# Two attentions of a twelve-stage block run as one sequence of places, with their heads' preparation put last in each place

## What is computed

```python
qa = (rmsnorm(cq, cq_gain) @ w_uq).reshape(lead + (8, 64 + 32))
kv = (rmsnorm(ckv, ckv_gain) @ w_ukv).reshape(lead + (8, 64 + 64))
ka = jnp.concatenate([kv[..., :64], kr_h], axis=-1)   # kr_h: kr for all 8 heads
qa, ka = rmsnorm(qa, q_gain), rmsnorm(ka, k_gain)      # "mla": 8 heads, 8 key heads
qb, kb = rmsnorm(gq, qg_gain), rmsnorm(gk, kg_gain)    # "gqa": 8 heads, 2 key heads
qa, ka = rope_tail(qa, 32, row, col), rope_tail(ka, 32, row, col)
oa = joint_dense_attention(qa, ka, va, kac, vac)       # 512 tokens see 768 keys
ob = joint_dense_attention(qb, kb, vb, kbc, vbc)       # context sees its 256
x = x + gate * ((concatenate([oa, ob]) * silu(g)) @ w_out)
```

## Time and profile before

| | us |
|---|---|
| median of 3 runs | 1555.17 (1554.95 to 1555.58) |
| the profiled execution, its own time | 1554.78 |
| its span | 1553.0 |
| PE busy | 1487.5 (96%) |
| DVE busy | 850.9 (55%) |
| ACT busy | 677.9 (44%) |
| POOL busy | 592.3 (38%) |
| chain that ended last, share by PE | 81% |

### The profile page before, as it was taken

How to read it: one execution, slowest core, us unless ns; L and a number is a source line. 1 busy time by engine, 2 the same in 40 slices (tenths; PEclk the granted TensorE clock), 3 DMA queues, 4 the chain that set the end, 5 groups by cost and what they waited for, 6 DMA issues and landing times.

```text
span 1553.0 us, 25078 instructions
## 1 busy us (share of the span) xinstructions
PE 1487.5 (96%) x9488; PEld 1240.5 (80%) x9488; DVE 850.9 (55%) x1879; ACT 677.9 (44%) x1377; POOL 592.3 (38%) x349
## 2 busy tenths in 40 slices
PE   4999998898999999999899999999999999999998
PEld 3778787787888878888788889967788788877887
DVE  4573708876764265933742997056322599617322
ACT  3333336565566353335744333467323433346332
POOL 1212223691005553447725444423234444430244
PEclk9999999999999999999999999999999999999999
DMA  9657620000012333331013323300233233310322
GB/s 326 181 140 192 175 62 27 2 2 1 2 35 89 108 109 96 95 95 42 28 33 94 96 82 98 93 14 28 69 93 106 75 99 101 96 41 1 109 82 95
DMA packets 103717, 128.61 MB, mean 83 GB/s; under 512 B 10608, under 2 KB 63792, under 8 KB 103600
## 3 DMA queue, kind: packets, MB, share of 16 engines
q1 hardware_dynamic: 103600, 127.01, 27.4%
HBM read 124.90 MB, written 2.10 MB: 82 GB/s over the span
## 4 chain that ended last, share of the span: by engine, by line
PE 81%; DVE 7%; POOL 5%; ACT 3%; issue 3%; DMA 1%; SPq 1%; DVEq 0%; ACTq 0%; POOLq 0%
PE psum L1048 21%; PE psum L1050 20%; PE psum L1049 20%; PE psum L1293 3%; PE psum L1236 3%; PE psum L1004 2%; PE psum L1215 2%; PE psum L1151 1%; PE psum L1340 1%; PE psum L1322 1%; PE psum L1272 1%; POOL rx L2403 1%; POOL mla_q L2403 1%; DVE psum L1943 1%; PE psum L1273 1%
## 5 line engine op out<-in xcount | busy, mean ns | idle before, releaser
L2353 POOL TENSOR_TENSOR wlo<-wraw,whi 128x1024 fp32r<-128x1024 f32 (+4 forms) x181 | 413.1, 2283 | 704.6 <-ACT whi L1445 704.6
L1445 ACT ACTIVATE whi<-wraw 128x1024 fp32r<-128x1024 f32 (+4 forms) x181 | 181.6, 1003 | 421.7 <-PE psum L1050 415.4
L1048 PE MATMUL psum<-whi,h2h 128*128 128x512 f32 (+2 forms) x800 | 309.5, 387 | 2.6 <-DVE h2l L1959 1.5
L1050 PE MATMUL psum<-whi,h2l 128*128 128x512 f32 (+2 forms) x800 | 305.2, 382 | 0.0
L1049 PE MATMUL psum<-wlo,h2h 128*128 128x512 f32 (+2 forms) x800 | 304.6, 381 | 0.0
L1048 PEld LDWEIGHTS psum<-whi,h2h 128*128 128x128 f32 x800 | 150.3, 188 | 28.5 <-issue 2.7
L1050 PEld LDWEIGHTS psum<-whi,h2l 128*128 128x128 f32 x800 | 150.2, 188 | 27.1
L1049 PEld LDWEIGHTS psum<-wlo,h2h 128*128 128x128 f32 x800 | 150.4, 188 | 24.8
L1048 PE MATMUL psum<-whi,hTh 128*128 128x512 f32 (+2 forms) x372 | 143.4, 385 | 3.7 <-DVE hTl L1959 2.7
L1050 PE MATMUL psum<-whi,hTl 128*128 128x512 f32 (+2 forms) x372 | 136.2, 366 | 0.0
L1049 PE MATMUL psum<-wlo,hTh 128*128 128x512 f32 (+2 forms) x372 | 135.8, 365 | 0.0
(11 more groups left out here) (391 smaller groups left out, 2956.4 us busy)
## 6 DMA issues: line engine op xcount, KB each, us to landing
rx<-mod_w_in SPq DMA_DIRECT2D x32, 512.0 KB, 5.1
wraw<-w_in_odd_in SPq DMA_DIRECT2D x32, 512.0 KB, 3.6
wraw<-cd_w_in_in SPq DMA_DIRECT2D x24, 512.0 KB, 3.7
wraw<-w_in_even_in SPq DMA_DIRECT2D x20, 512.0 KB, 3.7
wraw<-ab_w_out_in SPq DMA_DIRECT2D x16, 512.0 KB, 3.7
wraw<-w_ple_gate_in SPq DMA_DIRECT2D x16, 512.0 KB, 3.8
mod_w_even<-mod_w_in SPq DMA_DIRECT2D x8, 512.0 KB, 10.3
wraw<-ab_w_in_in SPq DMA_DIRECT2D x8, 512.0 KB, 8.3
```

Source lines behind the costliest of these rows:

```text
L1048: eng.matmul(dst, a[0], ww[0], start=first, stop=False)
L1050: mm = eng.matmul(dst, a[1], ww[0], start=False, stop=last_)
L1445: eng.activation(hi_of(u)[:, :, 0:w], wraw[:, u["id"] % RAW, :, 0:w], ACT.Copy).then_inc(*to("split_hi", u["id"]))
L2353: eng.tensor_tensor(lo_of(u)[:, :, 0:w], wraw[:, u["id"] % RAW, :, 0:w], f32(hi_of(u)[:, :, 0:w]), ALU.subtract)\
```

## The change

1. gqa and mla are one sequence: `places(*names)` gives 96 places and four more, and every engine's loop runs over it, so that mla's first scores stand where gqa's last probabilities are turned.
2. In a place ACT now does copy, exponential, then the high part of the preparation; DVE does maximum, copy, gate, inverse, then the low part, then `beside`. This holds for win too.
3. In mla's first block the preparations stand in places 3 to 10.
4. Key sums: POOL squares only the 64 columns that differ from head to head, in 12 half tiles with two buffers, and the shared 32 once; DVE sums two half tiles per place, behind the maximum. The key gain's first 64 columns are folded into the query gain, and POOL multiplies the keys by the gain in 32 columns only. Keys come before queries on POOL.
5. A key preparation of gqa waits only for the doubled keys, a query preparation for the queries; the first ones of mla wait for the tiles that they turn.
6. Modulation tiles 30 and 31 leave in1 for gqa's places 0 to 2.
7. diff, fox and odd wait for their values at their first product with them.
8. Slabs 0 to 3 of out3 and out4 are turned in fox and odd.
9. fox's scores use banks 0, 2 and 3 in turn. The second spread in win stands at place 6 instead of 9.

```diff
+        def mod_bank(n_):
+            return 6 if n_ == 31 else 7
...
         def mods_beside(n_):
-            return (2 * n_ - 8, 2 * n_ - 7) if 4 <= n_ < 4 + len(MOD) // 2 else ()
+            return mod_pair(n_) if n_ < 19 else ()
...
-                     ("win", 3): (1, 0, 0), ("win", 9): (1, 0, 1)}
+                     ("win", 3): (1, 0, 0), ("win", 6): (1, 0, 1)}
...
-        late_turns = {"fox": "m3", "odd": "m4"}
+        late_turns, EARLY_SLABS = {"fox": "m3", "odd": "m4"}, 4
...
-            groups = groups_of(late_turns[name], 0, 2)
+            groups = groups_of(late_turns[name], 0, EARLY_SLABS)
...
+        def places(*names):
+            return [(name, j) for name in names for j in range(len(units_of(name)) + 4 * (name == names[-1]))]
+        def product_of(place):
+            return place[0], place[1] // 2
...
+        def pair_scores(n_):
+            return 2 * (n_ % 2) if PAIR[n_][0] == "diff" else (0, 2, 3)[n_ % 3]
...
-                    when = first + (3 * before // 2 if name == "mla" else 2 + 2 * before)
+                    when = first + (max(3 * before // 2, 3 + before if first == 0 else 0) if name == "mla" else 2 + 2 * before)
...
# tensor
+            def start_modulation(j):
+                if j < 2:
+                    modulation_tile(30 + j)
+                if j > 0:
+                    turn_modulation(29 + j)
...
-                if p_[0] == prep_times(name)[-1][0][0]:
+                if name in STACKED and key[1] == 0:
+                    for w_ in [("keys_twice", (name, 1))] if key[0] == "k" else [("vector", ("normed", name[0] + "q", t)) for t in tiles]:
+                        eng.wait_ge(*at(*w_))
+                elif p_[0] == prep_times(name)[-1][0][0]:
...
+                if name == "mla" and key[1] == 0:
+                    for t in tiles:
+                        eng.wait_ge(*at("gpsimd", ("normed", "m" + key[0], t)))
...
# scalar, column_attention
-                for j in range(len(units) + 4):
+                for n_, (name, j) in enumerate(seq):
...
+                    if 2 <= n_ < len(seq) - 2:
+                        copy_probs(*seq[n_ - 2], turned_probs(*seq[n_ - 2]), product_of(seq[n_ - 5]) if n_ >= 5 else None)
+                    if j < len(units):
+                        if n_ >= 3:
+                            probs_free(*seq[n_ - 3])
+                        exponentials(name, j, probs(name, j))
                     for what in preps_at(name, j):
                         prep(*what)
-                    if 2 <= j < len(units) + 2:
-                        copy_probs(name, j - 2, turned_probs(name, j - 2), (name, (j - 5) // 2) if j >= 5 else None)
-                    if j < len(units):
-                        if j >= 3:
-                            probs_free(name, j - 3)
-                        exponentials(name, j, probs(name, j))
...
# vector: the low parts (`low`) move behind copy, gate and inverse in the same way
...
+            def reduce_keys(n_):
+                half_, t = divmod(n_, NT)
+                a = NT * 8 + t * 8 + half_ * 4
+                eng.wait_ge(*at("squares_g", ("mk", n_)))
+                after_last()
+                eng.tensor_reduce(ssq[:, a:a + 4], key_squares(n_), AX.X, ALU.add).then_inc(*note("vector", ("reduced", "mk", n_)))
...
# gpsimd, mla_norms
+                for n_ in range(2 * NT):
+                    half_, t = divmod(n_, NT)
+                    eng.wait_ge(*at("evac_act", (f"up{2 + half_}", t)))
+                    if n_ >= 2:
+                        eng.wait_ge(*at("vector", ("reduced", "mk", n_ - 2)))
...
-                for name, roots in (("mq", heads_rstd[:, 0:48]), ("mk", heads_rstd[:, 48:96])):
+                for name, roots in (("mk", heads_rstd[:, 48:96]), ("mq", heads_rstd[:, 0:48])):
```

More of the change, by code:

```diff
@@ L764, in heads_view, with key_squares @@
             return ap.rearrange("p (h d) -> p h d", h=h)
+        shared_squares = squares[:, 512:512 + NT * 32].rearrange("p (t d) -> p t d", t=NT)
+        def key_squares(n_):
+            return squares[:, n_ % 2 * 256:n_ % 2 * 256 + 256].rearrange("p (h d) -> p h d", h=4)
         norms = {
@@ L1194, in _ @@
             ready_of = {
-                "gqa": [("keys_twice", ("gqa", 1))] + [("vector", ("normed", "gq", t)) for t in ALL],
-                "mla": [("gpsimd", ("normed", n_, t)) for n_ in ("mq", "mk") for t in ALL] + [evac_of("up3", t) for t in ALL],
-                "win": [("keys_twice", ("win", 1))] + [("vector", ("normed", "wq", t)) for t in XT],
+                "mla": [evac_of("up3", t) for t in ALL],
                 "diff": [("vector", ("normed", n_, t)) for n_ in ("qa", "ka") for t in XT],
@@ L1244, in copies_ready, with column_attention @@
                     eng.wait_ge(*at("probs_b", (name, i)))
-            def column_attention(name):
-                units, preps = units_of(name), prep_times(name)
-                n_units, waited = len(units), set()
-                for j in range(n_units + 3):
-                    if j < n_units:
+            def column_attention(*names):
+                seq, waited = places(*names), {name: set() for name in names}
+                for n_, (name, j) in enumerate(seq[:-1]):
+                    units = units_of(name)
+                    if j < len(units):
                         h, t = units[j]
-                        wait_heads(name, j, waited)
+                        wait_heads(name, j, waited[name])
                         s0 = score_bank(j)
@@ L1345, in pair_attention @@
             def pair_attention():
-                for name in ("diff", "fox"):
-                    for n_ in values_of[name]:
-                        for t in XT:
-                            eng.wait_ge(*at(*evac_of(n_, t)))
                 waited = set()
@@ L1416, in _ @@
             products("up")
-            column_attention("gqa")
-            column_attention("mla")
+            column_attention("gqa", "mla")
             products("out1")
@@ L2104, in copy_probs, with column_attention @@
                 eng.tensor_copy(place[:, 0:nb * P], psum[:, 4, 0:nb * P]).then_inc(*note("probs_a", (name, i)))
-            def column_attention(name, beside=lambda j: None):
-                units, preps = units_of(name), prep_times(name)
-                for p_ in preps[-1] if name == "win" else ():
-                    first_head(name, p_)
-                for j in range(len(units) + 4):
-                    if j < len(units):
-                        maximum(name, j)
+            def column_attention(*names, beside):
+                seq = places(*names)
+                for p_ in prep_times("win")[-1] if "win" in names else ():
+                    first_head("win", p_)
+                for n_, (name, j) in enumerate(seq):
+                    if j < len(units_of(name)):
+                        maximum(name, j)
+                    if 2 <= n_ < len(seq) - 2:
+                        copy_probs(*seq[n_ - 2], turned_probs(*seq[n_ - 2]), product_of(seq[n_ - 5]) if n_ >= 5 else None)
+                    if n_ >= 5 and n_ % 2:
+                        name2, m = product_of(seq[n_ - 5])
+                        z = gate_columns(name2, m)
+                        eng.wait_ge(*at("product_v", (name2, m)))
+                        eng.tensor_tensor(z, psum[:, 6, P:2 * P], z, ALU.mult).then_inc(*small())
+                        after_last()
+                        eng.tensor_tensor(z, psum[:, 6, 0:P], z, ALU.mult).then_inc(*note("mixed", (name2, m)))
+                    if n_ >= 3 and n_ % 2 and n_ < len(seq) - 1:
+                        name2, m = product_of(seq[n_ - 3])
+                        eng.wait_ge(*at("exps", (name2, 2 * m + 1)))
+                        c_, r_ = 2 * m % 4, 2 * (m % 4)
+                        eng.reciprocal(rinv[:, r_:r_ + 2], rsum[:, c_:c_ + 2]).then_inc(*note("vector", ("inverse", name2, m)))
@@ L2124, in column_attention @@
[L2124 to L2129 removed]
+                    if name != "mla":
+                        beside(j)
             def attention(name):
@@ L2283, in _ @@
                     first_head("gqa", p_)
-            column_attention("gqa", mla_norms)
-            column_attention("mla")
+            column_attention("gqa", "mla", beside=mla_norms)
             products("out1", 0)
@@ L2306, in conv @@
                        .then_inc(*note("conv", ("lo", c)))
-            column_attention("win", conv)
+            column_attention("win", beside=conv)
             products("out2")
@@ L2402, in mla_norms @@
                         turned = t in XT
-                        eng.tensor_tensor(view(t), view(t), gg, ALU.mult).then_inc(*(small() if turned else note("gpsimd", ("normed", name, t))))
+                        part = view(t)[:, :, first:d]
+                        eng.tensor_tensor(part, part, gg, ALU.mult).then_inc(*(small() if turned else note("gpsimd", ("normed", name, t))))
                         if turned:
```

139 lines of the change are left out of this document (83 added, 56 removed).

## The result

| | us |
|---|---|
| before, median of 4 (lowest, highest) | 1555.38 (1554.95, 1555.97) |
| after, median of 4 (lowest, highest) | 1577.62 (1575.97, 1579.04) |
| ratio after/before, 95% interval | 1.0143 (1.0128 to 1.0159) |
| profiled execution of after, its span | 1575.97, 1574.1 |

The kernel became slower by 22.2 us. The sign is the one that I gave, and the chain through bank 7 is what the profile shows; but the size is twice what I gave (22.2 against 10.1), and 1577.6 lies outside the range of 1549 to 1574.

What follows compares the result with a forecast made beforehand. PE's instruction stream and its waits were taken to bound the kernel. Costs of 21.1 us less gains of 11.0 gave +10.1 on 1554.78, so 1564.9, against the median some 1565; range 1549 to 1574.

Steps and rivals of the forecast that it cites:

- the chain through bank 7: End of gqa and mla: each close preparation waits for the previous low part; costs 21.1 us, total 1565, chance 0.58.
- The eight preps: mla's first head preparations, in gqa's places 40 to 47: their starts spread from 16.35 to 23.3 us, costing +6.9.
- blocks two and three: mla's second and third block: three neighbouring pairs of preparations in each take longer, +3.6 per block, +7.2 together.
- the row of seam, copies and first block: From gqa's drain through mla's first block: seam -2.8, copies ahead of the low part -1.0, first block +7.0; +3.2 together.
- Rival B: gqa places 40 to 47: low parts not late enough to hold PE, kernel faster at 1543 us; chance 0.15.
- C: Part of both: early copies remove gqa's 3.9 us idle, start gains 4 more; 1557, down to 1551; chance 0.15.
- I take 0 for gqa's middle and win together, between -4 and +4: Preparations stand two or more places apart, bank 7 free in time; a late copy traded for a later one, net 0.
- Three banks for fox: -0.5: fox's first score waits for a later exponential of diff, the following ones for an earlier one; -0.5 us.
- Four early slabs: -1.5: Slabs 2 and 3 turned inside fox and odd, removing the first product's wait of 1.5 us for h2l; -1.5.
- The start: First key preparation, modulation pair and key sums at gqa's start: -1.2 us, between 0 and -5.
- rival D: Clock falls to 1.2 GHz over gqa's end and mla's first block, or win's waits double; 1573 to 1581, chance 0.12.
- The sign that it stays at 1.00: In the profile after, the granted clock was to stay at 1.00; the sum had no term for it.

Runs made afterwards that it cites:

- k1_late_mla: The changed kernel with preparation parts last in a place for mla's heads alone, first for gqa's own and win's; 1569.54 us (1.0091).
- e1_early: The changed kernel with both parts of the heads' preparation back at the front of a place, on ACT and DVE; 1550.83 us (0.9967).
- e3_dve_early: The changed kernel with the low part back right behind the maximum on DVE alone, the high part still behind the exponential; 1603.30 us (1.0311).
- g1_best_slabs2: The changed kernel with high parts first, low parts early for mla only, fox's three banks starting with bank 0, two early slabs; 1542.70 us (0.9918).
- e7: The kernel before with one part of the change only, both preparation parts last in a place; 1584.12 us (1.0181).
- f2: The changed kernel with preparation parts first on both engines and fox's scores in banks 0 and 2 in turn; 1546.42 us (0.9944).
- f3: The changed kernel with preparation parts first on both engines and fox's three banks starting with bank 0; 1546.64 us (0.9944).
- e6: The changed kernel, late parts kept, with fox's scores in two banks as before the change; 1574.98 us (1.0123).
- h1: The kernel before with only the preparations of mla's first block moved to places 3 to 10; 1555.57 us (1.0003).

## Why the prediction was right in sign and short in size

*The chain through bank 7: right.* The eight preps over 23.77 us (predicted 22 to 24, sum 23.3); the waits of L1261 at 20.5 (15 to 20); blocks two and three +3.4 each (+3.6). k1_late_mla, by medians, puts the whole at 18.7 where the sum gave 21.1. That the row of seam, copies and first block is right (+3.3, +3.2) is partly luck: e1_early, without the order's cost, gains 2.2 there where the sum had 2.8, which leaves 5.5 for the order where the sum had 7.0 less 1.0 for the copies. Rival B, lo parts that are not late enough, fell at the first of these numbers; C with it.

*"I take 0 for gqa's middle and win together, between -4 and +4": the step that failed first.* It measured +5.8 by medians, outside its own bounds. I had seen that DVE would wait one place further on and that PE would wait there instead, and took the exchange as even. For the copies it nearly is (5.1 us of PE's waits for them against 4.7). What failed is the premise that in gqa "bank 7 is free in time": PE waits there 1.7 us for lo where it waited 0, 0.5 more at the gated products, and a stretch at half clock comes with the order. In win, 1.1 us by the profiles, PE's waits for DVE's copies and for ACT's exponentials grow; which link leads there was not taken apart. (Another 0.4 of that row, at 968 us, comes and goes between the profiles whatever the order.)

*"Three banks for fox: -0.5": wrong sign, +2.6 to +4.3.* The text named the later exponential for which the first score waits, and set it against savings later in fox. There was one, of 0.7 us, and it came back at the turn of slab 2, where PE waits for POOL instead.

*"Four early slabs: -1.5": wrong sign, +2.2.* The wait for h2l at out3's start does go. But PE meets POOL's normalized rows at slab 2, 2.0 us too early, and "ACT and DVE do the same roundings earlier" left out that odd has no room for them: by the matched profiles its end loses 2.1 us with four slabs early and 0.8 to 0.9 with two.

*The other gains: right or too small.* POOL -1.6 (-1.4), diff's values -1.4 and odd's -1.5 (together -2.6 predicted). The start gave -3.8 (-1.2, "between 0 and -5"). None of these was undone by itself; they are read from the stages of the profiles. Up to fox, e1_early is 9.1 us ahead of before.

*The clock: my sum had no term for it, and rival D's was another one.* The sign that it stays at 1.00 failed. D put half clock over the end of gqa as a whole, at 8 to 16 us; that the measured 1577.6 lies between D's 1573 and 1581 is chance. What the traces show is single stretches of 3.4 us: one in the kernel before, three in the changed one, nine in e3_dve_early, which waits most, none inside g1_best_slabs2, which waits least. They stand near places where PE had stood still. By the Trainium skill (TensorE: Matmul & The Clock Gate, Terms) time at half rate costs half of its length; an estimate worked out from that for three of them is 5.1 us at the most. The second cost less: the step in which it ends is 0.4 longer than in e7, since bank 7's chain, not PE, sets most of the time there. The Trainium skill's rule that frequent short pauses between groups bring such dips (TensorE: Matmul & The Clock Gate, A second HAM failure mode) agrees in kind with these counts of 1, 3, 9 and 0, which are one profile each.

The sum of the wrong steps is about the miss: 4.1+1.3 in gqa and win, 4.3 in fox and out3, 1.5 in odd and out4, 1.5 at the start-up (the clock, same code) and 0.9 at the very end, less 2.6 at the start of gqa: 11.0, as 21.1-10.1.

## What to carry to other kernels

Work that feeds a single buffer (here one PSUM bank for all preparations) belongs ahead of the long operation of its place, on every engine of its chain; moved behind it, it costs the long operation's time at every step. Where a chain runs over two queues, never let its first link be late while its last stands early: hi late with lo early was the worst of the four orders (1603.3), both late came next (1577.6), while lo late alone cost 6.3 us (1557.1). When a buffer's rotation changes, ask of the *first* use in the new rotation for whom it waits, since this is all that the third bank changed; and turn a bundle of edits over one by one, for here three that cost (the order, the third bank, the slabs) stood beside others that pay, and a third kernel with the paying ones was 35 us below the bundle.

## What the runs showed that I had not expected

A wait can cost more than its length. Around the 2.8 us that fox's first score waits in e1_early, PE runs 6.8 us at 1.2 GHz; with a wait of 0.8 (f2, f3, g1) it does not. In the changed kernel, with the same 2.8, the clock holds there and falls 26 us later, behind the 2.0 for POOL. This probably decides, too, how far runs of one kernel lie apart: 6.6 us in e1_early, 1.2 in g1_best_slabs2; the two pairs of e6's runs, 4 us apart at a clock of 0.993 and 0.996 to 0.997, point the same way. The start-up's 1 us would fit how the runs of one kernel fall into two groups: of the 18 runs of the kernel before beside e1_early, 9 lie from 1554.75 to 1555.19 and 9 from 1555.94 to 1556.63. What sets the clock is not settled by these runs.

The last transfer of the output takes longer in the changed kernel and in its variants (profiles of after, f2 and g1, with the same four instructions as before): the slowest of four lands 4.1 us after its issue, against 3.3 before. From the start of the last matmul to the end of the span it is 6.4 to 6.5 us in every profile of the changed kernel and its variants, and 5.5 to 5.6 in before, e7 and h1. First the line for the kernel before, then the one for g1_best_slabs2, from the view of that instruction:

```profile
DMA to landing us min/median/max: 2.6/2.9/3.3
```

```profile
DMA to landing us min/median/max: 2.6/3.0/4.1
```

That is 0.8 of the 0.9 us behind the last matmul. Its cause was not tried.
